# Attention: the sums of squares one half product later on TensorE

## The chip, the cores and the metric

One core of one Trainium2 chip. The metric is the device time of one execution in microseconds.

## What is computed

Two blocks of two layers each on a sequence of 256 tokens of width 1024, in float32. The change touches the attention of the second block (16 heads of 64, so that one block of 256 keys holds the whole sequence and only the causal part is left):

```python
q, k, v = jnp.split(h @ w_qkv, 3, axis=-1)
q = rms_norm_2(to_heads(q), q_norm_g)      # x * rsqrt(mean(x*x) + 1e-6) * g, per head
k = rms_norm_2(to_heads(k), k_norm_g)
s_own = jnp.einsum('bhqd,bhsd->bhqs', qc, k_own) * scale
s_own = jnp.where(dist_own >= 0, s_own - slopes * dist_own, -jnp.inf)
p = jax.nn.softmax(scores, axis=-1)
out = jnp.einsum('bhqs,bhsd->bhqd', p_own, v_own)
return out @ w_o
```

## The kernel before, in words

Activations lie transposed: 128 features on the partitions, 256 tokens along a row. Every weight comes from memory in slots of 1024 x 256 (RAW), is split by ACT into a high part (WH, line 628) and by DVE into the rest (WL, line 661), and TensorE adds three matmuls for each tile of 128 x 128: high by high, high by low, low by high. A slot makes a product of two **half products** of 24 matmuls (`half`, lines 427 to 429; for the values `half_tok`, lines 443 to 445). There are three slots of each kind, so slot s + 3 can be split once slot s has been multiplied.

The order of the work on each engine is written out by hand. In attention, TensorE goes through the products of q and k, by turns, for four groups n of 256 columns, then through four products of v. The first pair, q and k of group 0, comes in one ramp ahead. After every half product the program takes one step (`run_steps`) in each generator of a list: one `pe_att(pe, n, done)` for each group of q and k, started after k's product n, and one `pe_values(pe, n, done)` for each product of v, started after it. An older generator's step comes first. ACT and DVE have lists of the same kind, with two steps for every whole product.

For a group n of q and k (four heads), the steps pass from engine to engine:

- ACT squares (line 1853) and takes the high part (line 1855); DVE takes the low part, **low(n)** (line 2117);
- TensorE adds the squares with a matrix of ones, **sum(n)**: four matmuls of 512 columns, lines 954 and 955 (`pe_square_sum`), into PSUM banks 3 and 4;
- ACT loads a table (line 1857) and takes the logarithms, **Ln(n)**: two operations of line 1863; later the exponential of line 1866;
- DVE scales q and k, **n(n)**: two of line 306 on 128 x 512;
- TensorE makes the **scores(p)** of head pairs p = 2n and 2n + 1 (lines 1216 and 1217, into the same banks 3 and 4); DVE takes them out (two of line 306 on 128 x 384) and finds the maxima; ACT takes the exponentials (lines 1875 and 1876); DVE divides by the sums (lines 2748 to 2751, **sc(p)**);
- TensorE transposes, **turn(p)** (line 310); ACT copies the result (line 1885); TensorE multiplies by the values, **pv(p)** (line 1251), which also needs ACT's copy of the product of v (line 1968).

On ACT the order around Ln(n) for n = 1 to 3 is: exponentials of pair 2n - 2, table, Ln(n), split of a weight slot (line 628), copy of a product (line 1968), copies of turn(2n - 2), exponential of line 1866, exponentials of pair 2n - 1, the next split.

After the four products of v the output product (`ao`) starts with a ramp that needs all eight head pairs, and a layer of feed-forward products ends the program.

Both versions of `pe_att` start with a step that issues nothing. Behind the sum, before:

```python
pe_square_sum(pe, b, ONE64, 8 + m).then_inc(S.att.pe.tick("sum", n, m), 1)
yield
yield
yield
```

Of the kernel before, what the change touches and what calls it, by code (L numbers as in the profile page):

```python
# [205 lines left out]
def program(nc, xT, wst, wad, cols, rows, crow, pT, cst, late, out, plan):  # L206
# [11 lines left out]
    with ctx:  # L218
# [89 lines left out]
        def tr(pe, o, a):  # L308
            n = a.shape[0]
            return pe.transpose(o, a, cs("ident", 0, n, n))  # L310
# [4 lines left out]
        def vacate(pe, b, *point):  # L315

            n = S.bank[b].fill(*point)
            if n:
                pe.wait_ge(S.bank[b].sem, n)
# [89 lines left out]
        def blk(m):  # L409
            return slice(m * 128, (m + 1) * 128)  # L410
# [541 lines left out]
        def pe_square_sum(pe, b, ones, a):  # L952

            pe.matmul(two(b), ones, YH[:, a:a + 2, :], start=True, stop=False)
            return pe.matmul(two(b), ones, YL[:, a:a + 2, :], start=False, stop=True)
# [243 lines left out]

        def pe_att(pe, n, done):  # L1200
            yield
            pe.wait_ge(*S.att.ve("low", n))
            for m in range(0, 4, 2):
                b = 3 + m // 2
                vacate(pe, b, "sum", n)
                pe_square_sum(pe, b, ONE64, 8 + m).then_inc(S.att.pe.tick("sum", n, m), 1)
            yield
            yield
            yield

            def scores(p):
                for hh in range(2):
                    c = 4 * n + p % 2
                    q, k = AQ[64 * hh:64 * hh + 64, c, :], AQ[64 * hh:64 * hh + 64, c + 2, :]
                    vacate(pe, 3 + hh, "s", p)
                    pe.matmul(PS[3 + hh][:, 0:128], q[:, 0:128], k[:, 0:128], start=True, stop=True)
                    pe.matmul(PS[3 + hh][:, 128:384], q[:, 128:256], k, start=True, stop=True).then_inc(S.att.pe.tick("s", p, hh), 1)

            def turn(p):
                sc = SCB[p % 2]  # L1220
                pe.wait_ge(*S.att.ve("sc", p))
                for hh in range(2):
                    vacate(pe, 5 + hh, "pt", p)
                    for q in range(3):
                        t = tr(pe, PS[5 + hh][:, blk(q)], sc[:, hh, blk(q)])
                    t.then_inc(S.att.pe.tick("tr", p, hh), 1)
                done.add(p)

            pe.wait_ge(*S.att.ve("n", n))
            scores(2 * n)  # L1230
            yield
            yield
            scores(2 * n + 1)
            turn(2 * n)
            yield
            yield
            turn(2 * n + 1)
# [22 lines left out]
        def tensor_program(pe):  # L1260
# [46 lines left out]
            bg, done = [], set()  # L1307
            open_ramp(pe, "r2", [("at", 0, 0), ("at", 1, 0)])
            bg.append(pe_att(pe, 0, done))
            for w, n in QK[2:]:  # L1310
                for m in range(2):
                    half(pe, ("at", w, n), XHL, 0, m, (lambda k: pe.wait_ge(*S.al("r2", k))) if (w, n) == QK[2] else None)
                    run_steps(bg)
                if w:
                    bg.append(pe_att(pe, n, done))
# [1602 lines left out]
```

## Time and profile before

| | us |
|---|---|
| median of 3 runs | 1287.3 |
| lowest and highest | 1284.98, 1287.5 |
| the profiled execution | 1285.15 |
| its span | 1283.4 |
| TensorE busy (matmul) | 1263.7 |
| VectorE (DVE) busy | 977.6 |
| ScalarE (ACT) busy | 753.3 |
| attention, first half product to the output product | 985.3 to 1074.5 |

A time on a row is counted from the span's start. A matmul's length overlaps the next one's, so rows follow each other at less than their lengths: what a half product takes is the distance of starts. Idle time in brackets is that of the engine ahead of the row, and behind the arrow stands what ended it. Releasers are inferred.

### The profile page before, as it was taken

How to read it: one execution, taken by the hardware profiler on the slowest of the kernel's cores; microseconds unless marked ns; L12 is line 12 of the kernel's file. 1: busy time of each engine (PE TensorE's matmuls, PEld its weight loads, DVE VectorE, ACT ScalarE, POOL GpSimd, SP SyncE). 2: the span in 40 equal slices, each digit the busy share in tenths (PEclk: the TensorE clock that was granted, in tenths of full speed). 3: DMA queues.
4: the chain of work that ended last, by engine and by line, in shares of the span. 5: the costliest groups of instructions: out<-in, count | busy, mean ns of one | idle time of the engine just before them, and what ended most of it. 6: DMA issues, size and time to landing. Idle time of an engine off the chain costs nothing.

```text
span 1283.4 us, 29824 instructions
## 1 busy us (share of the span) xinstructions
PE 1263.7 (98%) x12986; PEld 1150.0 (90%) x12986; DVE 977.6 (76%) x1539; ACT 753.3 (59%) x1027; POOL 28.3 (2%) x66
## 2 busy tenths in 40 slices
PE   9999999999999999999999999999999999999998
PEld 9999899999899999998987779888888988988887
DVE  5878768666878888886767988898787775886543
ACT  6766344474665655654564157876346885778431
POOL 0000000000000000000000000000000000000000
PEclk9999999999999999999999999999999999999999
DMA  8553445545476555654332245688874332665552
GB/s 313 181 180 130 162 170 180 209 172 191 170 284 223 212 198 201 218 208 165 132 131 101 100 157 198 238 320 312 313 268 160 136 132 99 244 252 210 189 189 66
DMA packets 34946, 247.51 MB, mean 193 GB/s; under 512 B 3904, under 2 KB 3904, under 8 KB 5504
## 3 DMA queue, kind: packets, MB, share of 16 engines
q1 hardware_dynamic: 29104, 204.96, 43.6%
q0 software_dynamic: 5712, 40.63, 8.7%
q8 instruction: 103, 1.69, 0.5%
q14 instruction: 27, 0.22, 0.0%
HBM read 244.53 MB, written 1.05 MB: 191 GB/s over the span
## 4 chain that ended last, share of the span: by engine, by line
PE 83%; DVE 9%; ACT 5%; issue 2%; POOL 0%; DVEq 0%; ACTq 0%; POOLq 0%
PE PS L511 17%; PE PS L427 9%; PE PS L512 9%; PE PS L428 8%; PE PS L429 8%; PE PS L528 5%; DVE WL L661 3%; ACT WH L628 2%; PE PS L443 2%; PE PS L1125 2%; PE PS L445 2%; PE PS L444 2%; DVE BIG L306 2%; PE PS L510 1%; PE PS L1057 1%
## 5 line engine op out<-in xcount | busy, mean ns | idle before, releaser
L661 DVE TENSOR_TENSOR WL<-RAW,WH 128x2048 fp32r<-128x2048 f32 x166 | 380.0, 2290 | 103.7 <-ACT WH L628 100.2
L628 ACT ACTIVATE WH<-RAW 128x2048 fp32r<-128x2048 f32 x166 | 316.8, 1909 | 144.5 <-PE PS L512 66.2
L427 PE MATMUL PS<-XW,WH 128*128 128x256 f32 x928 | 270.8, 292 | 0.2 <-DVE X L306 0.2
L428 PE MATMUL PS<-XW,WH 128*128 128x256 f32 x928 | 262.8, 283 | 1.1 <-issue 1.1
L429 PE MATMUL PS<-XW,WL 128*128 128x256 f32 x928 | 262.6, 283 | 0.2 <-issue 0.2
L427 PEld LDWEIGHTS PS<-XW,WH 128*128 128x128 f32 x928 | 177.5, 191 | 4.4 <-issue 1.8
L428 PEld LDWEIGHTS PS<-XW,WH 128*128 128x128 f32 x928 | 177.9, 192 | 1.4 <-issue 1.3
L429 PEld LDWEIGHTS PS<-XW,WL 128*128 128x128 f32 x928 | 177.7, 192 | 0.0
L511 PE MATMUL PS<-XW,WH 128*128 128x512 f32 x392 | 141.0, 399 | 0.2
L511 PE MATMUL PS<-YW,WH 128*128 128x512 f32 x368 | 129.9, 395 | 0.0
L306 DVE SCALAR_TENSOR_TENSOR BIG<-BIG,C 128x256 f32<-128x256 f32 (+2 forms) x232 | 103.0, 505 | 9.9 <-ACT BIG L1352 5.3
L512 PE MATMUL PS<-XW,WL 128*128 128x256 f32 x392 | 110.2, 281 | 0.0
L512 PE MATMUL PS<-YW,WL 128*128 128x256 f32 x368 | 103.3, 281 | 0.0
L651 DVE CUSTOM_DVE_ANT_0 BIG<-BIG,CB 128x1024 f32<-128x1024 f32 x76 | 90.1, 1224 | 0.0
L511 PEld LDWEIGHTS PS<-XW,WH 128*128 128x128 f32 x392 | 73.8, 188 | 16.4 <-DVE WL L661 0.8
L511 PE MATMUL PS<-HX,WH 128*128 128x512 f32 x240 | 84.9, 394 | 0.0
L511 PEld LDWEIGHTS PS<-YW,WH 128*128 128x128 f32 x368 | 69.0, 188 | 14.8
L512 PEld LDWEIGHTS PS<-XW,WL 128*128 128x128 f32 x392 | 74.2, 189 | 2.3
L528 PE MATMUL PS<-BIG,RAW 128*128 128x256 f32 (+1 forms) x320 | 74.1, 384 | 0.0
L528 PEld LDWEIGHTS PS<-BIG,RAW 128*128 128x128 f32 x320 | 59.5, 190 | 13.4 <-issue 5.8
L512 PEld LDWEIGHTS PS<-YW,WL 128*128 128x128 f32 x368 | 69.6, 189 | 1.0
L512 PE MATMUL PS<-HX,WL 128*128 128x256 f32 x240 | 67.2, 280 | 0.0
(447 smaller groups left out, 2570.2 us busy)
## 6 DMA issues: line engine op xcount, KB each, us to landing
RAW<-wst SPq DMA_DIRECT2D x191, 1024.0 KB, 4.8
BIG<-wad POOLq DMA_DIRECT2D x38, 1024.0 KB, 5.2
X<-xT SPq DMA_DIRECT2D x2, 512.0 KB, 4.8
RAW<-wst SPq DMA_DIRECT2D x2, 512.0 KB, 6.6
outT<-X SPq DMA_DIRECT2D x4, 256.0 KB, 4.2
K<-cst SPq DMA_DIRECT2D x1, 608.0 KB
CB<-crow SPq DMA_DIRECT2D x1, 512.0 KB
BIG<-pT POOLq DMA_DIRECT2D x2, 256.0 KB, 4.4
```

Source lines behind the costliest of these rows:

```text
L306: return ve.scalar_tensor_tensor(out=o, in0=a, scalar=s, in1=b, op0=op0, op1=op1)
L427: pe.matmul(o, h, hl[0][:, k0 + k, :], start=(k == 0), stop=False)
L428: pe.matmul(o, h, hl[1][:, k0 + k, :], start=False, stop=False)
L429: t = pe.matmul(o, l, hl[0][:, k0 + k, :], start=False, stop=(k == 7))
L443: pe.matmul(o, h, wh[:, k, :], start=(k == 0), stop=False)
L444: pe.matmul(o, h, wl[:, k, :], start=False, stop=False)
L511: pe.matmul(two(b + n), h, op, start=start, stop=False)
L512: return pe.matmul(PS[b + n][:, 0:T], l, op[:, 0, :], start=False, stop=False)
L528: t = pe.matmul(o, w[:, k, n * 128:(n + 1) * 128], op(k), start=(k == 0), stop=(k == 7))
L628: ac.activation(WH[p % NS][:, :], RAW[u % NR][:, :], ACT.Copy).then_inc(S.hi.tick(p), 1)
L651: t = ve.tensor_tensor_reduce(out=w, in0=w, in1=CB1[:, :], scale=1.0, scalar=0.0, op0=ALU.mult, op1=ALU.add, accum_out=MOD[:, 2 * n + m:2 ...
L661: ve.tensor_tensor(WL[p % NS][:, :], RAW[u % NR][:, :], WH[p % NS][:, :].bitcast(f32), ALU.subtract).then_inc(S.lo.tick(p), 1)
```

## The change

One `yield` moves from behind the sum to ahead of it. In each of the four groups sum(n) is issued at the third step rather than the second; scores(2n) stays at the fifth.

```diff
         def pe_att(pe, n, done):
             yield
+            yield
             pe.wait_ge(*S.att.ve("low", n))
             for m in range(0, 4, 2):
                 b = 3 + m // 2
                 vacate(pe, b, "sum", n)
                 pe_square_sum(pe, b, ONE64, 8 + m).then_inc(S.att.pe.tick("sum", n, m), 1)
-            yield
             yield
             yield
```

The rows on the other engines are the same in the same order. On TensorE, sum(1) leaves its place between the two half products after scores(0):

```order
 L428 MATMUL PS<-XW,WH 128x256
 L429 MATMUL PS<-XW,WL 128x256
-L954 MATMUL PS<-YW,HX 128x512
-L955 MATMUL PS<-YW,HX 128x512
-L954 MATMUL PS<-YW,HX 128x512
-L955 MATMUL PS<-YW,HX 128x512
 L427 MATMUL PS<-XW,WH 128x256
 L428 MATMUL PS<-XW,WH 128x256
```

It comes back one half product on, and there the older generator's step, scores(1) and turn(0), stands ahead of it:

```order
 L1217 MATMUL PS<-BIG 128x256
 L310 MATMUL PS<-K,BIG 128x128 x6
+L954 MATMUL PS<-YW,HX 128x512
+L955 MATMUL PS<-YW,HX 128x512
+L954 MATMUL PS<-YW,HX 128x512
+L955 MATMUL PS<-YW,HX 128x512
 L427 MATMUL PS<-XW,WH 128x256
 L428 MATMUL PS<-XW,WH 128x256
```

So sum(1) has moved past a half product, scores(1) and turn(0). sum(2) moves in the same way; sum(0) moves past a half product alone. At the values, sum(3) lands between turn(4) and the first product with the values, pv(0), whose rows are L1251:

```order
 L1217 MATMUL PS<-BIG 128x256
 L310 MATMUL PS<-K,BIG 128x128 x6
+L954 MATMUL PS<-YW,HX 128x512
+L955 MATMUL PS<-YW,HX 128x512
+L954 MATMUL PS<-YW,HX 128x512
+L955 MATMUL PS<-YW,HX 128x512
 L1251 MATMUL PS<-BIG 64x128 x6
 L443 MATMUL PS<-WH,XW 128x256
```

Before, pv(0) followed turn(4) at once, and sum(3) stood a half product earlier.

## Rows read from the trace of the kernel before

**Rows 1.** Waits of PE, 985 to 1075 us: line, releaser; total, times, longest.
```profile
PE PS L954 <- DVE YW L2117: 3.9, 4, 2.4
```

**Rows 2.** Timeline of PE, first squares' sum: start, length, operation, [idle <- releaser].
```profile
990.96 0.28 PE L429 MATMUL PS<-XW,WL 128*128 128x256 f32 x1
993.66 0.50 PE L954 MATMUL PS<-YW,HX 128*128 128x512 f32 x1 [2.42 <-DVE YW L2117]
...
994.69 0.28 PE L427 MATMUL PS<-XW,WH 128*128 128x256 f32 x1
```

**Rows 3.** Timeline of PE, scores(0), and the second squares' sum.
```profile
1003.41 0.50 PE L1216 MATMUL PS<-BIG 64*128 64x128 f32 x4
1003.74 0.61 PE L1217 MATMUL PS<-BIG 64*128 64x256 f32 x4
...
1007.13 0.28 PE L429 MATMUL PS<-XW,WL 128*128 128x256 f32 x1
1007.89 0.50 PE L954 MATMUL PS<-YW,HX 128*128 128x512 f32 x1 [0.48 <-DVE YW L2117]
...
1008.23 0.40 PE L955 MATMUL PS<-YW,HX 128*128 128x512 f32 x1
```

**Rows 4.** Timeline of PE, scores(1), turn(0), then turn(1), scores(2).
```profile
1011.90 0.50 PE L1216 MATMUL PS<-BIG 64*128 64x128 f32 x4
...
1012.76 0.87 PE L310 MATMUL PS<-K,BIG 128*128 128x128 f32 x6
...
1019.23 0.82 PE L310 MATMUL PS<-K,BIG 128*128 128x128 f32 x6
1019.98 0.50 PE L1216 MATMUL PS<-BIG 64*128 64x128 f32 x4
```

**Rows 5.** Timeline of DVE: n(0), scores(0), sc(0), sc(1), n(1).
```profile
1000.76 1.41 DVE L306 SCALAR_TENSOR_TENSOR BIG<-BIG,C 128x512 f32<-128x512 f32 x2
1004.45 1.02 DVE L306 SCALAR_TENSOR_TENSOR BIG<-BIG,PS 128x384 f32<-128x384 f32 x2 [2.27 <-PE PS L1217]
...
1010.50 0.69 DVE L2751 TENSOR_TENSOR BIG<-BIG,SM 128x512 f32<-128x512 f32 x1
...
1017.24 0.17 DVE L2748 RECIPROCAL SM<-SM 128x4 f32<-128x4 f32 x1
...
1018.39 1.41 DVE L306 SCALAR_TENSOR_TENSOR BIG<-BIG,C 128x512 f32<-128x512 f32 x2
```

**Rows 6.** Timeline of ACT, Ln(0), then Ln(1) and what stands around it.
```profile
995.46 1.26 ACT L1863 ACTIVATE BIG<-PS,EP 128x512 f32<-128x512 f32 x2
...
1008.42 0.19 ACT L1876 ACTIVATION_READ_ACCUMULATOR BIG<-BIG,SM 128x1 f32 x1
1008.63 1.28 ACT L1857 ACT_TABLE_LOAD   x1
1009.92 1.27 ACT L1863 ACTIVATE BIG<-PS,EP 128x512 f32<-128x512 f32 x2
...
1016.84 0.19 ACT L1876 ACTIVATION_READ_ACCUMULATOR BIG<-BIG,SM 128x1 f32 x1
```

**Rows 7.** Timelines of PE and ACT: scores(4), Ln(3), copy, pv(0), scores(6).
```profile
1036.57 0.50 PE L1216 MATMUL PS<-BIG 64*128 64x128 f32 x4
...
1043.09 1.27 ACT L1863 ACTIVATE BIG<-PS,EP 128x512 f32<-128x512 f32 x2
...
1046.04 0.59 ACT L1968 ACTIVATE BIG<-PS 128x512 f32<-128x512 f32 x1
...
1046.73 0.88 PE L1251 MATMUL PS<-BIG 128*64 128x128 f32 x12
...
1055.13 0.50 PE L1216 MATMUL PS<-BIG 64*128 64x128 f32 x4
```

**Rows 8.** Windows: length, busy of PE, PEld, DVE, ACT, POOL, PEclk, DMA.
```profile
985.00:1074.50 89.50, 83.81 (x709) 76.06 (x707) 66.90 (x107) 73.71 (x139) 0.00 (x0) 1.00 0.33 119
1074.50:1283.40 208.90, 204.96 (x1254) 182.47 (x1252) 129.65 (x143) 113.12 (x126) 2.10 (x4) 1.00 0.51 186
```


## The prediction

> **What bounds the kernel now.** I read the windows first: in attention TensorE is busy 83.81 of 89.5 us, and behind it, in the 208.9 us to the end, 204.96 [rows 8]. Anything that lets it run on counts, and anything that holds it up does too. A delay that attention hands on is therefore not made good later. Then TensorE's waits in attention: the four sums of squares wait for DVE's low part 3.9 us in all, 2.4 the first [rows 1]. That is the wait that the change moves away from. In the timeline the issue gap is what counts: the matmul before sum(0) starts at 990.96 and the next could follow 0.12 later, at 991.08; the sum starts at 993.66, so it holds TensorE for 2.58 us [rows 2]. Sum(1) could start at 1007.25 and starts at 1007.89, 0.64 late [rows 3]. Last I read the timelines of DVE and ACT across one group of heads, for what follows a sum. This shows how little room there is: DVE finishes n(1) at 1018.39 + 1.41 = 1019.80 [rows 5], and TensorE issues scores(2), which need it, at 1019.98 [rows 4]. DVE and ACT have idle time, but the chain through both of them ends only 0.18 us before it is needed.
>
> **The change, part by part.** No instruction is added or removed, and no DMA is moved. What changes is when the sums come, and so when ACT's Ln(n) can start, which waits for them.
>
> *Group 0.* The half product now issued ahead of sum(0) starts at 991.1. Half products cost 2.91 us each (three from 994.69 to 1003.41 [rows 2, 3]), so sum(0) starts near 994.0, when its operand is long there: no wait. ACT starts Ln(0) at 995.46, right behind its table load [rows 6], and the sum's first bank is ready before that, near 994.8, so ACT and DVE keep their times and n(0) ends at 1000.76 + 1.41 = 1002.17 [rows 5]. TensorE, now ahead, comes to scores(0) at 994.0 + 1.0 + 2 x 2.9 = 1000.8 and waits until 1002.2, against 1003.41 before [rows 3]. Of the 2.58 us **1.2 us are gained**; the rest becomes a wait for n(0).
>
> *One round.* Call t the start of scores(2n). Before, t to the next such start is 16.57 us (1003.41 to 1019.98 [rows 3, 4]). After, TensorE does scores (its successor is 0.86 behind it, 1011.90 to 1012.76 [rows 4]), then two half products with nothing between them. The first would end at t + 3.84 (1003.41 to 1007.25 [rows 3]), the second at t + 6.75. Scores(2n + 1) follow, until t + 7.61. Now turn(2n) needs DVE's sc(2n). DVE starts on scores(0) at t + 1.04 and ends sc(0) at 1010.50 + 0.69, 6.74 us later [rows 5]: t + 7.78. A wait of 0.2. Turn takes 0.75 (1019.23 to 1019.98 [rows 4]), so the sum starts at t + 8.58. The banks are no further wait: DVE takes scores(2n + 1) out of them in two operations of 1.02 together from t + 7.8, and the sum's second bank is wanted after t + 9.0. The sum's first bank is done 0.74 after its start (1007.89 to 1008.23 + 0.40 [rows 3]).
>
> How soon ACT answers no row shows, since ACT never waits for a sum before. From one side, DVE answers the last scores matmul (1003.74 + 0.61 = 1004.35 [rows 3]) at 1004.45, 0.10 later [rows 5]; from the other, that same answer comes 1.04 after the first scores row starts, which is 0.3 more than the 0.74 here. I take 0.10, since it is an answer to a finished matmul, and keep 0 and 0.3. So Ln starts at **t + 9.42**, where before it started at 1009.92, t + 6.51 [rows 6], with no idle time.
>
> Behind it on ACT, which works in order, stand a weight split, a product's copy, the copies of turn(2n), the second logarithm's exponential and the exponentials of pair 2n + 1. None of these waited before: from Ln's start to the end of the last accumulator row is 1016.84 + 0.19 - 1009.92 = 7.11 us [rows 6]. So these exponentials end at t + 16.53. DVE then divides (1017.24 to 1018.39, 1.15) and scales q and k (1.41 [rows 5]), with two answers of 0.05: t + 19.2. Scores(2n + 2) start then, where they started at t + 16.57. TensorE has finished its next two half products at t + 9.6 + 5.8 = t + 15.4, so it waits some 2.4 us for turn(2n + 1) and 0.6 more for n(n + 1). Each round **costs 2.6 us** in place of the 0.64 it saves. Two rounds of this kind, to scores(2) and scores(4): +5.2.
>
> *The third round* ends at scores(6), 18.56 us after scores(4) before (1036.57 to 1055.13 [rows 7]). Here pv(0) stands straight behind sum(3), and it needs ACT's copy of the product of v, which stands on ACT behind Ln(3) and a weight split: from Ln's start to the copy's end is 1046.04 + 0.59 - 1043.09 = 3.54 us [rows 7]. So pv(0) starts at t + 9.42 + 3.54 + 0.05 = t + 13.0, after a wait of 3.5 us. From pv(0) to scores(6) TensorE ran 8.40 us without waiting (1046.73 to 1055.13 [rows 7]); ACT's and DVE's chains (t + 9.4 + 7.4 + 2.6, with the copy of pv(0) in it) end before. Scores(6) start at t + 21.4: **+2.8**. With sum(3) over, the rest of attention has the same order and the same chain as before, shifted.
>
> Slots: the split behind Ln(1) on ACT is for a product that starts over 10 us later, and the loads are released by DVE's splits up to 3 us later with as much room; so I cost both at nothing. What covers them is that distance of two products, 11.6 us; if it were gone, TensorE would wait for the split by the same 2.9 us by which Ln is late.
>
> *Sum:* -1.2 + 5.2 + 2.8 = **+6.8 us**. Against the profiled execution, 1285.15 (span 1283.4), that is 1291.9; but that run lies 2.2 us below the median of the three, two of which agree at 1287.3 and 1287.5. I put the difference on the median: **1294.1 us**.
>
> One price a page disputes. ACT's table load ends at 1008.63 + 1.28 = 1009.91 and Ln(1) starts at 1009.92; ahead of the load the accumulator row ends at 1008.61 [rows 6]. Nothing but the load's 1.28 us is paid. The Trainium skill, "ScalarE: Activation LUTs", section "What ACT_TABLE_LOAD costs", gives 1.28 us for the load and about 1.38 us of drain on top for each switch. Hidden under the new wait, three such drains would be an estimate of 4.1 us won back, and the sum +2.7; the trace disagrees, so I leave it out.
>
> **The rivals.**
>
> *The waits just vanish (faster).* All four gaps go and nothing takes their place, because ACT and DVE have room: 2.58 + 3 x 0.64 = 4.5 us, 1282.8. For it: DVE idles 2.27 us ahead of scores(0) [rows 5]. Against it: the chain from Ln(1) through ACT to n(1) has 0.18 us of room [rows 4, 5], and Ln comes 2.9 later against scores(2n). It decides from the point at which Ln comes no more than 0.2 us later. Chance 0.03.
>
> *A wash.* ACT makes up most of the late start, so each round loses about what the first group gains: within 2.6 us of 1287.3. It would need ACT's 7.11 us to shrink, and they hold no idle time. Chance 0.05.
>
> *A smaller loss.* The values product's copy doesn't hold pv(0) as computed, and only the ordinary wait is paid in the third round, about +1.0 there: 1287.3 + 5.0 = 1292.3. The order of ACT speaks against it. Chance 0.15.
>
> *The clock falls.* The granted clock is 1.00 of 2.4 GHz across all of attention, after a gap of 2.42 us as well [rows 2, 8], but TensorE would now wait 2.4 and 0.6 near each other, and 3.5 in one. No row has the lower level, 1.2 GHz; at most it doubles a half product, +2.9 each. Two half products at it would give 1294.1 + 5.8 = 1299.9. The Trainium skill, "TensorE: Matmul & The Clock Gate", Part 1, says that throttled is the default state and that activity releases it, so by that rule a long wait can bring the clock down; no row here shows a wait of that length. Chance 0.06.
>
> **How the numbers follow.** My own case has 0.71: 1294.1, between 1291.3 and 1297.3. Below, each of the three rounds costs 0.6 less (Ln answered at once, and no 0.2 for sc(2n) and the like), 1.8, and the median comes out 1 us lower. Above, the answer takes 0.3 three times (0.6 more), some twelve waits hand over 0.15 late each (1.8), and the median lies 0.8 higher. The range is **1290.3 to 1297.3**: its lower end takes in the smaller loss, 1292.3, at the profiled run's level, 2 us lower. It leaves out the clock, the wash and the faster case. What a measurement can tell from no change is 0.2%, 2.6 us. Faster 0.03; the same 0.06, from the wash and a sliver of the smaller loss; slower 0.91.
>
> **What the changed profile would show.** Waits of L954 for L2117 gone, or nearly. Scores(0) about 1.2 us earlier, held by n(0) on DVE (line 306). ACT waiting about 2.9 us ahead of line 1863 in three groups, for line 955. TensorE waiting about 2.4 us ahead of line 310 in two groups (for line 2751), 0.6 us ahead of line 1216, and about 3.5 us ahead of line 1251 once, for line 1968. Starts of scores(2n) 19.2 us apart, then 21.4. The output product near 1081.3 in place of 1074.5. If ACT shows no wait for line 955, or rounds stay at 16.6 us, the reasoning is wrong; if all are as said and the time is not, something behind attention gives it back.

## The result and the profile after

The changed kernel is slower: a median of 1296.56 us (1294.96 to 1297.01, 4 runs) against 1286.74 (1284.98 to 1287.5, 4 runs), a ratio of 1.0076 with a 95% interval of 1.0059 to 1.0093. That is 9.8 us. Beside the experiments below it was timed again, at 1297.08 against 1286.31, a ratio of 1.0087 (1.0073 to 1.0101), 10.8 us. The profiled execution has a span of 1295.2 us, 11.8 more than before. A part of that, 1.3 us, lies ahead of attention, which starts at 986.6 instead of 985.3, and comes from no changed instruction; over all the profiles shown here this start lies between 985.1 and 987.6. Attention to the output product took 1086.3 - 986.6 = 99.7 us, before 89.2: 10.5 more. Where executions are compared below, it is by this stretch.

From the page of the changed kernel, the busy time of TensorE and the granted clock in tenths by slice:

```profile
PE 1268.6 (98%) x12986; PEld 1153.1 (89%) x12986; DVE 977.7 (75%) x1539; ACT 752.9 (58%) x1027; POOL 28.3 (2%) x66
...
PEclk9999999999999999999999999999999989999999
```

TensorE is busy for 4.9 us more with the same matmuls, and one slice of the clock has a digit lower than 9. Both say that part of the loss is no wait. Next, what TensorE waits for in attention (us in total, times, longest), where L954 for L2117 stood before [rows 1], beside the wait of L1251 for L2769 at the end, which is unchanged:

```profile
PE PS L310 <- DVE BIG L2751: 4.4, 2, 2.2
PE PS L1251 <- ACT BIG L1968: 3.2, 1, 3.2
PE PS L1216 <- DVE BIG L306: 2.2, 3, 1.4
PE PS L1251 <- DVE YW L2769: 1.7, 1, 1.7
```

The sums' waits are gone, all four. In their place stand the transposes of turn(1) and turn(3) (line 310), pv(0) (line 1251, for ACT's copy of line 1968) and the scores (line 1216). No product waits for a weight split. TensorE's timeline across the first round answers to [rows 3, 4]:

```profile
1003.53 0.50 PE L1216 MATMUL PS<-BIG 64*128 64x128 f32 x4 [1.42 <-DVE BIG L306]
...
1010.34 0.50 PE L1216 MATMUL PS<-BIG 64*128 64x128 f32 x4
...
1011.37 0.87 PE L310 MATMUL PS<-K,BIG 128*128 128x128 f32 x6
1012.00 0.48 PE L954 MATMUL PS<-YW,HX 128*128 128x512 f32 x1
...
1021.12 0.87 PE L310 MATMUL PS<-K,BIG 128*128 128x128 f32 x6 [2.20 <-DVE BIG L2751]
1022.45 0.50 PE L1216 MATMUL PS<-BIG 64*128 64x128 f32 x4 [0.45 <-DVE BIG L306]
```

Scores(0) waited 1.42 us for n(0), turn(1) 2.20 for sc(1), scores(2) another 0.45 for n(1), and scores(2) start 18.92 us after scores(0), where it was 16.57. What they waited for stands in rows that answer to [rows 5, 6], on ACT:

```profile
1008.75 1.28 ACT L1857 ACT_TABLE_LOAD   x1
1012.80 1.27 ACT L1863 ACTIVATE BIG<-PS,EP 128x512 f32<-128x512 f32 x2 [2.77 <-PE PS L955]
1013.96 1.92 ACT L628 ACTIVATE WH<-RAW 128x2048 fp32r<-128x2048 f32 x1
...
1019.59 0.21 ACT L1876 ACTIVATION_READ_ACCUMULATOR BIG<-BIG,SM 128x1 f32 x1
```

and on DVE:

```profile
1019.83 0.18 DVE L2748 RECIPROCAL SM<-SM 128x4 f32<-128x4 f32 x1 [1.63 <-ACT BIG L1876]
...
1020.99 1.41 DVE L306 SCALAR_TENSOR_TENSOR BIG<-BIG,C 128x512 f32<-128x512 f32 x2
```

ACT has loaded its table by 1010.03 and stands until 1012.80; the sum's first bank is done 0.74 behind 1012.00, so ACT answers within 0.06 us. From there to the end of the exponentials (1019.59 + 0.21) are 7.00 us without a gap, and behind them DVE's division and n(1) follow at once. The chain is the one predicted, down to its length. Its third round answers to [rows 7]. On ACT, Ln(3) and the copy of the product of v:

```profile
1053.47 1.27 ACT L1863 ACTIVATE BIG<-PS,EP 128x512 f32<-128x512 f32 x2 [4.81 <-PE PS L955]
...
1056.42 0.60 ACT L1968 ACTIVATE BIG<-PS 128x512 f32<-128x512 f32 x1
```

and on TensorE pv(0) and scores(6):

```profile
1057.07 0.93 PE L1251 MATMUL PS<-BIG 128*64 128x128 f32 x12 [3.24 <-ACT BIG L1968]
...
1066.95 0.50 PE L1216 MATMUL PS<-BIG 64*128 64x128 f32 x4
```

The copy's end is 3.55 us behind the start of Ln(3), and pv(0) follows it 0.05 later.

What was not in the sum is the clock. From TensorE's timeline, two neighbours in the half product behind scores(4), and a later one:

```profile
1044.04 0.41 PE L444 MATMUL PS<-WL,XW 128*128 128x256 f32 x1
1044.25 0.41 PE L445 MATMUL PS<-WH,XW 128*128 128x256 f32 x1
...
1048.32 0.28 PE L443 MATMUL PS<-WH,XW 128*128 128x256 f32 x1
```

Windows of the same profile, with the granted clock in the third column from the end (1.00 is 2.4 GHz, 0.50 is 1.2 GHz):

```profile
1041.00:1047.00 6.00, 5.71 (x27) 4.92 (x27) 4.12 (x8) 4.34 (x12) 0.00 (x0) 0.50 0.06 23
1048.00:1057.00 9.00, 5.83 (x44) 4.63 (x42) 4.10 (x9) 4.19 (x6) 0.00 (x0) 1.00 0.31 117
1057.00:1061.00 4.00, 3.93 (x26) 3.70 (x27) 1.97 (x2) 3.73 (x13) 0.00 (x0) 0.59 0.00 0
1086.30:1295.20 208.90, 205.01 (x1255) 182.33 (x1252) 129.63 (x143) 113.12 (x126) 2.10 (x4) 1.00 0.52 186
```

From 1041 to 1047 the clock is at its lower level, and matmuls of 256 columns start 0.21 us apart instead of 0.12 (24 in 2.91 us, [rows 2, 3]); the later one takes 0.28 us again, not 0.41. The clock had come down right behind the wait for turn(3), of 2.21 us, and it came down again at pv(0), behind a wait of 3.24. The third round, from scores(4) to scores(6), took 25.52 us in place of 18.56. Behind attention nothing is given back: the last window has the 208.9 us that it had before [rows 8].

### The profile page after: what moved, and what is told of

Read it like the earlier page. It is cut to its first block, busy times and chain, and to the rows that moved or that the text cites. A ratio compares the mean times of both kernels' runs of the same rounds, so it can differ in the third digit from the quotient of the medians.

```text
span 1295.2 us, 29824 instructions
## 1 busy us (share of the span) xinstructions
PE 1268.6 (98%) x12986; PEld 1153.1 (89%) x12986; DVE 977.7 (75%) x1539; ACT 752.9 (58%) x1027; POOL 28.3 (2%) x66
## 4 chain that ended last, share of the span: by engine, by line
PE 80%; DVE 10%; ACT 7%; issue 3%; DMA 0%; SPq 0%; DVEq 0%; ACTq 0%
PE PS L511 17%; PE PS L512 9%; PE PS L427 8%; PE PS L428 7%; PE PS L429 7%; PE PS L528 5%; DVE WL L661 4%; ACT WH L628 3%; PE PS L443 2%; DVE BIG L306 2%; PE PS L444 2%; PE PS L445 2%; PE PS L1125 2%; PE PS L510 1%; PE PS L1057 1%
## 5 line engine op out<-in xcount | busy, mean ns | idle before, releaser
L628 ACT ACTIVATE WH<-RAW 128x2048 fp32r<-128x2048 f32 x166 | 316.8, 1909 | 143.9 <-PE PS L512 66.3
```

Of the source, the lines that this page charges most:

```text
L628: ac.activation(WH[p % NS][:, :], RAW[u % NR][:, :], ACT.Copy).then_inc(S.hi.tick(p), 1)
```

## The experiments

My theory: a late sum costs what stands behind Ln on ACT, and the extra over the predicted 6.8 us is the clock. The rivals: the late sum is dear by its place on TensorE or by the banks that it shares with the scores, and the extra is something else.

**Only sum(0) late.** The yield is moved for n == 0 alone:

```diff
             yield
+            if n == 0:
+                yield
             pe.wait_ge(*S.att.ve("low", n))
...
-            yield
+            if not (n == 0):
+                yield
             yield
             yield
```

> Only sum(0) is moved one half product on; sums 1 to 3 stand where they stood before the change. My theory (a late sum costs where ACT's Ln has no room, and only sum(0) has room): TensorE's first wait of 2.4 us goes, scores(0) wait 1.3 to 1.4 us for n(0) instead, the later groups run as before the change, 16.6 us apart; 1.2 to 1.3 us faster than before the change, and 11 us faster than the changed kernel. Rival (moving a sum costs by itself, through the banks it shares with the scores or through any wait put elsewhere): slower than before, by 1 us or more.

1284.33 us against 1286.96, ratio 0.9986 (0.9977 to 0.9994): 2.6 us faster by medians. Attention took 87.92 us, 1.28 less than before, as forecast. TensorE's waits there, beside the unchanged one at the end (lines added to a kernel shift its line numbers, here by three, so that L1219 is the line that was L1216):

```profile
PE PS L954 <- DVE YW L2120: 1.5, 3, 0.5
PE PS L1219 <- DVE BIG L306: 1.4, 1, 1.4
```

Three sums still wait for their low parts, and scores(0) wait 1.4 us. So moving this sum costs nothing by itself. That the medians differ by more than the 1.28 us is taken up below.

**Only sum(3) late.** The same with n == 3.

> Only sum(3) is moved. My theory: pv(0) stands behind sum(3) and waits 3.2 us for the copy that stands on ACT behind Ln(3); this round is 2.9 us longer at a full clock: +2.9 us on the kernel before. If one wait of 3.2 us is enough to bring TensorE's clock down, a further 1 to 2 us; if the clock fell in the changed kernel only because waits came close together, the granted clock stays 1.00 here. Rival (ACT's order does not matter, the loss comes from group 1 and 2): within 1 us of before.

1291.45 us, ratio 1.0039 (1.0026 to 1.0051): 4.5 us slower. Attention took 94.84 us, 5.6 more than before. TensorE's waits:

```profile
PE PS L954 <- DVE YW L2120: 3.4, 3, 2.4
PE PS L1254 <- ACT BIG L1971: 3.2, 1, 3.2
```

and two windows (the clock third from the end):

```profile
994.00:1003.00 9.00, 8.62 (x56) 8.24 (x57) 6.23 (x5) 6.84 (x8) 0.00 (x0) 0.81 0.58 205
...
1048.00:1057.00 9.00, 5.77 (x40) 4.95 (x39) 4.13 (x7) 7.25 (x16) 0.00 (x0) 0.81 0.15 62
```

The wait of pv(0) is there, 3.2 us, and the clock was low for a part of the window behind it. It was low once more, in the window from 994: there nothing is changed, and what precedes it is the wait of 2.4 us ahead of sum(0) that the kernel before has too. The 5.6 us can be told apart by the starts of scores, against stretches at a clock of 1.00. Up to scores(0) attention took 19.48 us, where the kernel before took 18.09: 1.4 us for the first fall. The first two rounds are unchanged, 16.57 and 16.55. From scores(5) to scores(6) it took 16.03:

```profile
1045.45 0.50 PE L1219 MATMUL PS<-BIG 64*128 64x128 f32 x4
...
1061.48 0.50 PE L1219 MATMUL PS<-BIG 64*128 64x128 f32 x4
```

In the run called "The clock kept" below, whose clock stays at 1.00, the same stretch took 14.52: 1.5 us for the second fall. That leaves 2.8 us for the late sum itself, near the 2.9 expected.

**Sums late, logarithms late.** The changed kernel, and ACT's Ln(n) moves one step on, ahead of its exponential:

```diff
             ac.preload_act_table_set(OPEN)
+            yield
             if n:
                 ac.wait_ge(*S.att.ve("n", n - 1))
...
-            yield
             ac.wait_ge(*S.bank[4]("sum", n))
             ac.activation(rs, rs, ACT.Exp, scale=-0.5).then_inc(S.att.ac.tick("rs", n), 1)
```

> The changed kernel, and on ACT Ln(n) moves behind the weight split, the product's copy and the copies of turn(2n - 2), right ahead of its exponential. My theory (what stands behind Ln on ACT is what makes the late sum dear): ACT no longer waits 2.8 us for the sum, the waits of line 310 for line 2751 and of line 1251 for line 1968 go, the clock stays at 1.00, rounds are 16.1 us long, scores(0) start some 2 us earlier than before the change: 3.5 us faster than before, 13 us faster than the changed kernel. Rival (the late sum is dear by its place behind scores and turn on TensorE, or by the banks): rounds stay near 19 us and the time near the changed kernel's.

1282.71 us, ratio 0.9970 (0.9960 to 0.9980): 4.3 us faster than before the change and some 14 faster than the changed kernel, with the same instructions in number and kind. ACT's timeline in the first round:

```profile
1008.43 1.91 ACT L628 ACTIVATE WH<-RAW 128x2048 fp32r<-128x2048 f32 x1
1010.25 0.58 ACT L1968 ACTIVATE BIG<-PS 128x512 f32<-128x512 f32 x1
1010.72 0.86 ACT L1885 ACTIVATE BIG<-PS 128x384 f32<-128x384 f32 x2
1011.47 1.28 ACT L1864 ACTIVATE BIG<-PS,EP 128x512 f32<-128x512 f32 x2
```

TensorE's waits in attention:

```profile
PE PS L1251 <- DVE YW L2769: 1.7, 1, 1.7
PE PS L1216 <- DVE BIG L306: 1.3, 3, 0.8
```

and attention as one window:

```profile
985.00:1072.00 87.00, 83.58 (x712) 76.00 (x710) 67.42 (x108) 73.93 (x140) 0.00 (x0) 1.00 0.35 123
```

The weight split, the product's copy and the copies of turn(0) (L628, L1968, L1885) now fill the time in which ACT stood, and Ln(1) starts without a wait. Rounds took 16.33 and 16.34 us, the third 18.01, and the clock stayed at 1.00. TensorE's order is that of the changed kernel, row for row, with the same banks. That settles the first rival: the place on TensorE is good, and the order on ACT made it dear.

Not all of the 4.3 us is the new order's. Attention took 86.38 us, 2.8 less than in the profile of the kernel before: 1.8 up to scores(0) and 1.0 over the three rounds. The rest lies in the median of the kernel before, which is above its profiled execution; it is taken up below. The late logarithms can't be had without the late sum. On paper, with the sum in its old place, scores(1) wait for a bank that Ln(1) frees, Ln(1) stands on ACT behind the copies of turn(0), and turn(0) stands on TensorE behind scores(1): a circle. So that combination was not run.

**The clock kept.** The changed kernel with idle matmuls, identity times a constant, in the waits:

```diff
             yield
             yield
+            if n < 2:
+                pe_idle(pe, 5)
             turn(2 * n + 1)
...
                 pt = PTA[p % 6]
+                if p == 0:
+                    pe_idle(pe, 7)
                 pe.wait_ge(*evicted(("at", 2, n)))
```

> The changed kernel with idle matmuls (identity times a constant, into a bank not in use) in the waits: five ahead of turn(1) and of turn(3), seven ahead of pv(0), each 0.43 us; their results are used by nothing. My theory (chain of waits 6.8 us, the rest of the 9.8 us is the clock that falls to 1.2 GHz in two stretches): the same starts, granted clock 1.00 throughout, 3 to 3.5 us faster than the changed kernel, 6.5 us slower than before. Rival (the extra comes from something else, the clock being a bystander): the time of the changed kernel, or slower by what the matmuls take.

1291.89 us, ratio 1.0042 (1.0029 to 1.0056), 4.9 us slower than before and 5.2 faster than the changed kernel at 1297.08, which was timed on another chip; each against the kernel before on its own chip, it is 4.9 against 10.8. Attention as one window:

```profile
985.00:1082.50 97.50, 92.74 (x757) 83.57 (x755) 68.94 (x111) 74.31 (x142) 0.00 (x0) 1.00 0.33 112
```

and TensorE's waits in it that belong to the change:

```profile
PE PS L1216 <- DVE BIG L306: 2.3, 3, 1.4
...
PE PS L1255 <- ACT BIG L1972: 0.2, 1, 0.2
```

With the clock at 1.00 attention took 95.54 us, 6.3 more than before. The rounds were 18.92, 18.99 and 21.32 us, against 16.57, 16.59 and 18.56. That is near the sum that I had worked out, 6.8. In the profiled changed kernel the other 4.2 of the 10.5 us were the clock: 2.7 from scores(4) to scores(5) (9.50 us there, 6.80 here) and 1.5 from scores(5) to scores(6) (16.02 and 14.52):

```profile
1048.65 0.50 PE L1216 MATMUL PS<-BIG 64*128 64x128 f32 x4
...
1063.17 0.50 PE L1216 MATMUL PS<-BIG 64*128 64x128 f32 x4
```

By medians the loss is 4.9 us and not the 6.5 expected. The kernel before has executions with a low clock in its median. Executions with a mean granted clock of 1.000 give it without them: four of the five here have one, with a median of 1291.49 us, 6.7 over the 1284.80 of such executions of the kernel before (see below).

**Sum(1) and sum(2) late.** The same edit with n in (1, 2).

> Only sum(1) and sum(2) are moved. My theory: two rounds of 18.9 to 19.0 us in place of 16.6, with the waits of line 310 for line 2751 (2.2 us) and of line 1216 for line 306 (0.45); the third round as before, 18.6; attention 4.7 us longer at a full clock, and the time 4.7 us over before, with the clock's own 1.5 us if it falls. The parts then add up: 4.7, the last sum's 2.8 and the first sum's -1.3 make 6.2, against the 6.3 us by which attention with the kept clock was longer. Rival (the losses grow on each other, so that parts are not additive): 2 us or 8 us.

1293.49 us, ratio 1.0053 (1.0040 to 1.0066): 7.2 us slower. Attention took 97.13 us, 7.9 more; the rounds were 19.07 and 19.83, and 19.25 for the third. Windows behind its three waits of 2.4, 2.2 and 2.2 us:

```profile
994.00:1003.00 9.00, 7.69 (x48) 7.51 (x49) 6.31 (x4) 7.58 (x7) 0.00 (x0) 0.81 0.62 226
1022.00:1030.00 8.00, 5.85 (x36) 4.88 (x37) 5.08 (x11) 6.38 (x12) 0.00 (x0) 0.79 0.39 133
1042.00:1050.00 8.00, 5.74 (x35) 4.69 (x36) 5.25 (x11) 6.33 (x13) 0.00 (x0) 0.79 0.40 135
```

All three waits were followed by a stretch at the lower level, more than I had allowed for. The starts of scores show what each fall cost, against the same stretches at a clock of 1.00: 1.5 us up to scores(0) (19.58 and 18.09), 1.0 behind turn(1) (the first round 19.07 and 18.92, then scores(2) to scores(3) 7.66 and 6.81), 0.7 behind turn(3) (scores(4) to scores(5) 9.18, and 8.49 in the kernel before). These are 3.2 us, and 4.7 are left for the two late sums, as forecast. So the parts add up: 4.7, the last sum's 2.8 and the first sum's -1.3 make 6.2, against 6.3.

**The copy ahead of Ln(3).** The changed kernel, with ACT's copy of the first product of v before the exponentials of pair 4; the later copy is skipped:

```diff
+                if key == ("at", 2, 0):
+                    ac.wait_ge(*S.mm(key, 1))
+                    ac.activation(AV2[:, :, 0:256], two(bank_of[key]), ACT.Copy).then_inc(frees(key).tick(key, on="ac"), 1)
                 run_steps(bg)
+                if key == ("at", 2, 0):
+                    after(ac, key)
+                    bg.append(ac_values(ac, n, done))
+                    continue
```

> The changed kernel, with ACT's copy of the first product of v taken ahead of the exponentials of pair 4, the table and Ln(3), in place of behind them. My theory: pv(0) no longer waits for the copy (3.2 us before); the third round is about 19.3 us at a full clock in place of 21.3, the clock does not fall there, and may still fall after the wait for line 2751 ahead of turn(3). 4.3 us slower than before the change at a full clock, up to 2 more with one fall; 3.5 to 5.5 us faster than the changed kernel. Rival (the wait of pv(0) is only the place where the late sum shows, the chain behind it is as long): third round stays at 21 us or more.

1293.10 us, ratio 1.0051 (1.0039 to 1.0064): 6.8 us slower than before and 4.0 us faster than the changed kernel. The two pv at the end of the third round:

```profile
1053.19 0.88 PE L1251 MATMUL PS<-BIG 128*64 128x128 f32 x12
...
1058.54 0.88 PE L1251 MATMUL PS<-BIG 128*64 128x128 f32 x12 [1.41 <-DVE YW L2776]
```

Pv(0) follows sum(3) at once. But pv(1) then waits 1.41 us for y(0), the result of pv(0) on DVE (line 2776), which hangs on the same chain behind Ln(3) through ACT's line 1902. The round took 20.72 us with one fall of the clock at its start, behind turn(3), where I had expected 19.3 without a fall. From scores(4) to scores(5) it took 7.96 us, and 6.80 with the clock kept: 1.2 us for the fall. Less that, the round is 19.6, against 21.3. So about 1.7 us of the third round was the wait for the copy, not the 2.0 expected.

**The kernel before, with idle matmuls ahead of sum(0).** `pe_idle(pe, 5)` for n == 0 ahead of the wait for its low part.

> The kernel before the change, with five idle matmuls (2.2 us, results used by nothing) in the wait ahead of sum(0), which stays where it is. The start times of everything else should be the same. If the kernel before loses to the clock in part of its executions (its profiled one, at 1.00, was 1285.15 us with a median of 1287.0), this brings the median to 1285 to 1285.5, 1.5 to 2 us faster; if the spread comes from elsewhere, no change, within 0.5 us.

1285.60 us against 1286.31, ratio 0.9996 (0.9987 to 1.0004): by this alone unclear, and not the 1285 to 1285.5 that I expected. Attention took 89.16 us, as before, and the wait ahead of sum(0) is down to 0.26 us. The spread shows more. Its 11 runs lie between 1284.62 and 1286.79, the 15 of the kernel before between 1284.19 and 1288.53. And in 48 runs of the kernel before, beside these experiments, the 13 with a mean granted clock of 1.000 had a median of 1284.80 us, the 15 with 0.997 one of 1287.47 (the other 20, at 0.998 and 0.999, have medians of 1286.35 and 1287.05). With the idle matmuls none of the 11 runs has a clock under 0.999; of the 48 without, 21 have. The kernel before pays for the clock too, in many executions, and its profiled one happened not to. Some of that is ahead of attention: this kernel's clock, too, was low once, near 160 us, and so it was in four more of the profiles, behind waits of at most 1.4 us. The clock is not the whole spread: one of the 11, at a mean clock of 1.000, took 1286.79 us.

**The changed kernel again.**

> The changed kernel once more, beside the others on the same chip, for a second look at where the clock falls. If the fall needs only a wait of 2.2 us or more, every such wait should show one; if it depends on how the waits lie against something free-running, the falls are at other places than in the first profile (behind scores(4) and behind pv(0)) or their number differs. Time 9.5 to 10 us over before.

1297.08 us, 10.8 over the kernel before, where I had expected 9.5 to 10. Windows of its profile:

```profile
1012.00:1021.00 9.00, 6.79 (x54) 6.26 (x52) 4.88 (x7) 8.96 (x17) 0.00 (x0) 0.93 0.40 150
1021.00:1030.00 9.00, 9.00 (x68) 7.88 (x68) 6.84 (x11) 5.65 (x12) 0.00 (x0) 0.88 0.08 15
1039.00:1048.00 9.00, 8.03 (x43) 7.04 (x44) 7.12 (x10) 7.32 (x15) 0.00 (x0) 0.62 0.21 88
1057.00:1066.00 9.00, 9.00 (x73) 8.51 (x70) 5.40 (x8) 5.92 (x14) 0.00 (x0) 0.81 0.33 118
```

Here the clock was low behind turn(1) as well, across the border of the first two windows, and attention took 100.76 us. In the first profile it was not, with the same wait of 2.2 us ahead of it. So such a wait may bring the clock down and need not; what decides is not in these records. Over all the profiles with a late sum and no idle matmuls, the clock fell behind the 2.2 us ahead of turn(1) in two of four, behind the 2.2 us ahead of turn(3) in four of four, and behind the 3.2 us ahead of pv(0) in three of three.

**One table load.** On the version with late sums and logarithms, and on the kernel before, `if n == 0:` ahead of the table load, which leaves out three loads of 1.28 us.

> The version with late sums and late logarithms, and the table is loaded for group 0 alone (three loads of 1.28 us fewer on ACT; the set stays loaded between the groups). My theory: ACT then reaches Ln(n) up to 1.28 us sooner, but Ln waits for the late sum, so only about 0.3 us a group is won, the 0.28 and 0.22 us that scores(2) and scores(4) still wait for n(1) and n(2): 0.5 us faster than that version, about 4.5 to 5 us faster than before the change. Rival (the load is all room, or a drain of 1.4 us goes with it): no change, or 3 us and more.

1282.03 us against 1287.21, ratio 0.9962 (0.9949 to 0.9976). This is the lowest median, 5.2 us under the kernel before, but its interval overlaps that of the version without this edit (0.9960 to 0.9980), so the times alone do not tell the two apart. The rounds do. They took 16.04 and 16.09 us in place of 16.33 and 16.34, and scores(2) and (4) no longer wait for n(1) and n(2), for which they had waited 0.28 and 0.22 us in that version. ACT now waits for turn(0) ahead of its copies, and Ln(1) follows:

```profile
1010.23 0.88 ACT L1886 ACTIVATE BIG<-PS 128x384 f32<-128x384 f32 x2 [0.93 <-PE PS L310]
1011.09 1.27 ACT L1865 ACTIVATE BIG<-PS,EP 128x512 f32<-128x512 f32 x2
```

> The kernel before the change with the table loaded for group 0 alone. My theory: ACT's chain from Ln(n) starts 1.28 us sooner, but before the change TensorE never waits for n(1) to n(3), only for the low parts ahead of the sums, and these hang on the scores: n(1) ends earlier and TensorE's starts stay; within 0.5 us of before. Rival (ACT is on the path in the kernel before too): 2 to 4 us faster.

1286.91 us, ratio 0.9995 (0.9987 to 1.0004); rounds 16.57 and 16.55. Three loads fewer bring nothing there: TensorE's start times hang on the low parts ahead of the sums, and these on the scores. In the kernel before, DVE starts on scores(0) at 1004.45, works without a gap through low(1), which ends at 1007.84, and sum(1) starts at 1007.89.

## Why the prediction came out as it did

The direction was right, the chain of waits was right in kind and size, and the time lies inside the range, 2.5 us above the forecast of 1294.1. That last is in part luck: the range left the clock out, the clock took 4 to 5 us, and some 2 us of that were made up for by a base that was as much too high. By its steps:

- *Group 0.* 1.2 us gained, the rest a wait for n(0): measured 1.28 us in the run with sum(0) alone, with a wait of 1.40.
- *One round.* 19.2 us predicted, 18.92 and 18.98 measured. Turn(0) ahead of a sum takes 0.63 us (1011.37 to 1012.00) and not the 0.75 that I took from turn(1). ACT's answer took 0.06 us, near the 0.10. The queue behind Ln took 7.00 us, with 7.11 taken.
- *Third round.* 21.4 us, and 21.32 at a kept clock. The wait of pv(0), 3.5 predicted, was 3.24.
- *Slots.* Put at nothing, and no product waited for a split.
- *Sum.* 6.8 us, and 6.3 with the clock kept in the profile, 6.7 by executions at a mean clock of 1.000.
- *The rivals.* "The waits just vanish" fell at the first round, and for the reason given: with the logarithms moved, there was room, and then the late sums did make the kernel faster. "A smaller loss" fell with the wait of 3.24 us ahead of pv(0). "The clock falls" got 0.06 and was what happened, beside my own case and not in its place. **This is the step that failed**: I took the granted clock of 1.00 in the one profiled execution as a property of that wait of 2.4 us. It was one draw: the same wait brought the clock down in two other profiles. The rival had the right mechanism and a size of 5.8 us; it was 4.2 and, by 100.76 - 95.54, 5.2 us in the two profiles.
- *The base.* I added 6.8 us to the median of 1287.3. Executions at a clock of 1.000 have 1284.80, so some 2 us of that median go with a low clock, though not all of its spread does. For the profiled executions the account closes: 1285.15, 6.3 for the waits, 4.2 for the clock and 1.3 ahead of attention give 1296.95, and 1297.01 was measured. What the 1.3 us are no run shows.

The rule of the Trainium skill, "TensorE: Matmul & The Clock Gate", Part 1, that activity releases the throttle, agrees with this: filling the waits with idle matmuls kept the clock at 1.00. The Trainium skill, "ScalarE: Activation LUTs", section "What ACT_TABLE_LOAD costs", adds a drain of about 1.38 us to every switch to a different set. The three loads left out here load again the set that is already in use, so they don't test it, and the prediction's estimate of 4.1 us did not apply. In these loads no run shows a drain: without them a round of 16.33 us became 16.04, which the wait of 0.28 us ahead of scores(2) accounts for, and no more.

## What to carry to other kernels

Before a producer is issued later, look at the engine that consumes it and works in order: its own late start is less of a matter than all that is queued behind it, and here, but for the first group, the reordering paid only once both engines' orders were moved together. A chain that ends 0.2 us ahead of its use has no room, whatever idle time its engines show. Where TensorE gets waits like those here, of 2.2 to 3.2 us, price the clock as well, and read it in several executions, since one that shows it at 1.00 does not vouch for the next.

## What the runs showed of the hardware

- The clock came down behind waits of 2.2 and 2.4 us in some profiles and not in others for the same wait, and behind the wait of 3.2 us in all three that have it; ahead of attention it came down in five profiles behind waits of at most 1.4 us. A fall cost attention 0.7 to 1.5 us, the longer one behind turn(3), from 1041 to 1047, 2.7. At 1.2 GHz matmuls of 256 columns started 0.21 us apart, at 2.4 GHz 0.12, so at half the clock they took some 1.75 times as long.
- Idle matmuls in the waits cost nothing that can be seen: the first two rounds are as long with them (18.92 and 18.99 us) as without (18.92 and 18.98). With the clock that they kept attention was 4.2 us shorter than in one profile of the changed kernel and 5.2 than in the other.
